# Memory products of the second layer placed beside two norms of the first, and sums over x shared between VectorE and TensorE

## The chip, the cores and the metric

The kernel runs on one core of one Trainium2 chip. The metric is device microseconds of one launch, the median of several runs. A core has TensorE (PE in the rows; its weight loads are PEld), VectorE (DVE), ScalarE (ACT), GpSimd (POOL) and SyncE (SP), which here issues nearly all DMAs.

## The reference

One sequence of 256 tokens with 1024 features goes through a first block of two layers and then a second block of two layers. All is float32. The change touches the first block alone:

```python
x = layer_norm(x, emb_ln_g, emb_ln_b)                                   # norm 0
for l in range(2):
    x = layer_norm(alpha * x + hybrid_mixer(x, ...), ...)               # norm 1, norm 4
    x = layer_norm(alpha * x + memory_cross_attention(x, mem, ...), ...)  # norm 2, norm 5
    x = layer_norm(alpha * x + conv_ffn(x, ...), ...)                   # norm 3, norm 6

def memory_cross_attention(x, mem, xa_q, xa_kv, xa_o):                  # 4 heads of 256
    q = x @ xa_q * 256 ** -0.5
    k, v = split(mem @ xa_kv, 2)
    return (softmax(q @ k.T) @ v) @ xa_o
```

`k` and `v` are made from `mem`, which no layer changes, so these products of either layer depend on nothing that the first block computes. A layer norm needs, for each token, the sum over features of x and of x squared.

## The kernel before

Activations stand transposed, features on partitions: x is 128 x 8 x 256, held as four banks of 128x512. Every large product is cut into chunks, one for each weight piece of 1 MB (128x2048 float32). `plan` (line 105) writes the list of chunks, and all engines walk that list. For a chunk SP loads `raw` (ring of 5), ACT rounds it to `whi` (line 747), DVE subtracts to get `wlo` (line 1537), and PE makes three matmuls for each piece of 128x128 (hi by hi, hi by lo, lo by hi): 48 matmuls of 256 columns. So a chunk that PE multiplies at a given place was split some three chunks earlier (`LEAD`). A chunk may carry hooks: small pieces of other PE work issued ahead of one of its eight steps k.

The chunks of a layer: the mixer (`dq`, `dk`, ... `gate`, `branch`), then `mo` (ends with norm 1 or 4), then the memory attention: `xk` and `xv` (four each, the memory products, which read `memh` and `meml`), `xq` (four, which read the normed x), `xo` (four, which end with norm 2 or 5), then the feed-forward part `fu`, `fg`, `fo` (ends with norm 3 or 6). In both layers the order behind norm 1 or 4 is xk0 xv0 xk1 xv1 xq0 xk2 xq1 xk3 xq2 xq3 xv2 xv3: four memory products stand between the norm and the first chunk that needs its result. Behind norms 2 and 3 stands at once a chunk that needs it (`fu` 0; `dq` 0 of layer 1).

A layer norm runs through all engines:

1. DVE adds each of the four banks of product and x (line 1581). ACT squares each (line 771), DVE adds the squares (line 1574, `acc`).
2. PE sums over partitions by matmuls with ones (`norm_stats`): eight of 256 columns for x into `turnP`, two for `acc` and two for the last squares into `outP`. A float32 matmul shows as two instructions in the trace.
3. DVE takes each token's own sums (1663, 1665), makes mean and variance (1671 to 1673), POOL the power -0.5 (689), DVE two diagonals (1680, 1686), PE spreads them over the partitions (`norm_spread`).
4. For each bank DVE makes `cen` (1633, 1639), ACT the new x and its upper part `xh` (812, 816), and the lower part `xl` is made by DVE for the first bank (1653) and by POOL for the other three (694).

Where memory products follow (norms 1 and 4), `norm_stats` is a hook of the first of them (k = 5) and `norm_spread` one of the second (k = 1), and ACT and DVE make one split (`between`) ahead of the small statistics and one (`late`) ahead of the banks. Elsewhere PE issues both at once and waits, and the split comes behind the norm.

A head of the memory attention takes four steps: `scores` on PE, then its maximum on DVE and exponents on ACT; `turn`, transposes on PE and a copy `eT` on ACT (line 938); `mix`, PE, then a scaling on DVE; `back`, transposes on PE, then a split on ACT and DVE. Head j has its `scores` at the chunk of `xq` j plus 2, and each further step one chunk later.

Of the kernel before, what the change touches and what calls it, by code (L numbers as in the profile page):

```python
# [104 lines left out]
def plan():  # L105
# [15 lines left out]
    for l in range(DEPTH):  # L121
        base = len(chunks)
# [37 lines left out]
        add("M", "mem", l)  # L160
# [6 lines left out]
        for r, j in (("xk", 0), ("xv", 0), ("xk", 1), ("xv", 1), ("xq", 0), ("xk", 2), ("xq", 1), ("xk", 3),  # L167
                     ("xq", 2), ("xq", 3), ("xv", 2), ("xv", 3)):
            where[r, j] = add("T" if r == "xv" else "F", r, l, j)
# [4 lines left out]
        chunks[-1]["ends"] = norm  # L174
        for j in range(FG + 1):
# [17 lines left out]
        for pos, some in todo.items():  # L193
            steps[pos] = sorted(some, key=lambda s: order[s[0]])
# [34 lines left out]
def kernel_program(nc, xT, memT, consts, consts2, pos, par1, par2, bias, W, out):  # L229
# [3 lines left out]
    with ctx:  # L233
# [39 lines left out]

        part1 = ExitStack()
# [4 lines left out]
        qr = sb("qr", [P, 4, S], where=att)  # L279
        kr = sb("kr", [P, 4, S], where=att)  # L280
        qb = sb("qb", [P, 4, S], where=att)
        kb = sb("kb", [P, 4, S], where=att)
        va = sb("va", [P, 2, 512], where=att)
        vb = sb("vb", [P, 2, 512], where=att)
        att.close()
# [5 lines left out]
        hold = ExitStack()  # L291
        _skip = sb("skip_att", [P, 30 * 256], where=hold)
        gates = sb("gates", [P, 3, 4, S], where=hold)
        gbv = sb("gbv", [P, 2, S], where=hold)
        gcv = sb("gcv", [P, 2, S], where=hold)
        pc = sb("pc", [P, 2, S + 2], where=hold)
        cv = sb("cv", [P, 2, S], where=hold)
        mtmp = sb("mtmp", [P, 4, S], where=hold)
        hold.close()
# [7 lines left out]
        kx = sb("kx", [P, KT, S], where=xat)  # L307
        vx = sb("vx", [P, 2, D], where=xat)
# [6 lines left out]
        oxs.close()  # L315
        ff = ExitStack()
        fu = sb("fu", [P, 2, 512], where=ff)
# [7 lines left out]

        cc = sb("cc", [P, NC2], where=ff)
        cs2 = sb("cs2", [P, 2, S], where=ff)
        angle = sb("angle", [P, 2, S], where=ff)
        csr = angle
        posf = sb("posf", [P, S], where=ff)  # L330
        posi = sb("posi", [P, S], mybir.dt.int32, ff)
        q2 = sb("q2", [P, 2, 2, S], where=ff)
        k2 = sb("k2", [P, 2, 2, S], where=ff)
        v2 = sb("v2", [P, 2, 512], where=ff)
        up = sb("up", [P, 2, S], where=ff)
        pooled = sb("pooled", [P, 2, S], where=ff)
# [115 lines left out]
        norms = list(range(LAST + 1))  # L452
        ended = [n for n in norms if n not in (0, END1 + 1)]
# [5 lines left out]
        summed = sig("summed", [(n, b) for n in norms for b in range(1, NB - 1)])  # L459
        ystats = sig("ystats", [n for n in norms if n <= END1])  # L460
# [271 lines left out]
        def _(act):  # L732
# [41 lines left out]
            def norm(n, between=None, late=None):  # L774
# [12 lines left out]
                if between and (n > END1 or n % LNS == 1):  # L787
                    between()
# [32 lines left out]
                if between and n <= END1 and n % LNS != 1:  # L821
                    between()
# [5 lines left out]
            def take(c, pos):  # L828

                r, j, l = c["role"], c["j"], c["l"]  # L830
                if "ends" in c:

                    if c["role"] == "sd" and c["f"] == 0:
# [3 lines left out]
                         (lambda: split_at(pos + 3)) if c["role"] == "mo" else None)  # L837
# [258 lines left out]
        def _(pe):  # L1096
# [9 lines left out]
            def norm_stats(n):  # L1106

                outB.claim(pe, varied, n)
                if n <= END1:
                    turnB.claim(pe, ysums, n)  # L1110
                    for k in range(KT):
                        if k % 2 == 0:
                            await_x(pe, n, k // 2)
                        ins = mm(turnP[:, 0:S], ones[:, :], x[:, k, :], k == 0, k == KT - 1)
# [1192 lines left out]
```

## Time and profile before

| | us |
|---|---|
| median of 3 runs (lowest, highest) | 2185.16 (2183.87, 2185.5) |
| the profiled execution's own time | 2176.07 |
| its span in the trace | 2174.3 |
| PE busy in the span | 2093.7 |
| DVE busy | 1430.6 |
| ACT busy | 1004.3 |

The page gives busy time, then the share of the span. A busy PE is not PE at its peak: matmuls overlap, and the granted clock matters. In the second part of the page the span is cut into 40 slices, with one digit for each:

```profile
PE   7999999899989999998999799998999999999997
...
PEclk9999999999999999999999899999999999999999
DMA  5444554355534444534555355533555555533552
```

PE is at nine tenths or more nearly everywhere; the dips belong to the start, the norms and the end.

### The profile page before, as it was taken

The page shows a single profiled execution, that of the slowest core. Times are in us where ns is not written, and L with a number is a line of the kernel's source. Part 1 is how long each engine was busy: PE and PEld are TensorE (multiplying, and loading weights), DVE is VectorE, ACT ScalarE, POOL GpSimd, SP SyncE. Part 2 cuts the span into 40 slices and gives each one's busy share as a digit, 9 for nine tenths or more (in the row PEclk, how much of TensorE's full clock was granted, in tenths as well). Part 3 has the DMA queues.
Part 4 walks back from the last instruction along what each step waited for, and adds up shares of the span by engine and source line. Part 5 has one row for each costly group of instructions (what it writes and reads, how often), then busy time and mean ns, then how long its engine had stood idle before and what let it go on. Part 6 is the DMA issues. An engine that isn't in the chain of part 4 may idle for free.

```text
span 2174.3 us, 39332 instructions
## 1 busy us (share of the span) xinstructions
PE 2093.7 (96%) x17364; PEld 2038.1 (94%) x17364; DVE 1430.6 (66%) x1717; ACT 1004.3 (46%) x1166; POOL 53.2 (2%) x58
## 2 busy tenths in 40 slices
PE   7999999899989999998999799998999999999997
PEld 6899999899988999998999799988999999989997
DVE  6656564577765655646777766698666766887664
ACT  5554454444445444544444454444444544444442
POOL 1000000000000000001000000000000000000000
PEclk9999999999999999999999899999999999999999
DMA  5444554355534444534555355533555555533552
GB/s 206 151 160 159 190 177 154 117 194 194 194 120 155 156 175 175 192 139 147 193 194 194 104 193 195 190 136 119 194 194 194 180 194 192 178 130 132 194 195 83
DMA packets 52858, 365.95 MB, mean 168 GB/s; under 512 B 5904, under 2 KB 5904, under 8 KB 9296
## 3 DMA queue, kind: packets, MB, share of 16 engines
q1 hardware_dynamic: 52272, 361.21, 46.5%
q8 instruction: 138, 2.26, 0.4%
q0 software_dynamic: 416, 2.22, 0.3%
q14 instruction: 32, 0.26, 0.0%
HBM read 362.35 MB, written 1.05 MB: 167 GB/s over the span
## 4 chain that ended last, share of the span: by engine, by line
PE 82%; issue 9%; DVE 5%; ACT 2%; POOL 1%; DMA 1%; POOLq 0%; ACTq 0%
PE accM L1104 47%; PE scoreP L1104 18%; PE outP L1104 8%; PE turnP L1104 8%; DVE wlo L1537 1%; PE turnP L1284 1%; ACT ew L932 1%; ACT whi L747 1%; POOL small L689 1%; ACT x L812 0%; DMA raw<-in_W 0%; PE outP L1310 0%; DVE cen L1633 0%; DVE mrs L2076 0%; DVE cen L1639 0%
## 5 line engine op out<-in xcount | busy, mean ns | idle before, releaser
L1537 DVE TENSOR_TENSOR wlo<-raw,whi 128x2048 fp32r<-128x2048 f32 x336 | 768.4, 2290 | 379.7 <-ACT whi L747 379.1
L747 ACT ACTIVATE whi<-raw 128x2048 fp32r<-128x2048 f32 x336 | 640.1, 1911 | 261.9 <-PE accM L1104 143.6
L1104 PE MATMUL accM<-xh,whi 128*128 128x256 f32 x1152 | 337.2, 293 | 11.2 <-DVE xl L1653 10.7
L1104 PE MATMUL scoreP<-xh,whi 128*128 128x256 f32 x1152 | 323.1, 280 | 13.7 <-DVE xl L1653 8.8
L1104 PE MATMUL accM<-xh,wlo 128*128 128x256 f32 x1152 | 322.8, 280 | 0.0
L1104 PE MATMUL accM<-xl,whi 128*128 128x256 f32 x1152 | 322.8, 280 | 0.0
L1104 PE MATMUL scoreP<-xl,whi 128*128 128x256 f32 x1152 | 321.2, 279 | 0.0
L1104 PE MATMUL scoreP<-xh,wlo 128*128 128x256 f32 x1152 | 320.9, 279 | 0.0
L1104 PE MATMUL accM<-fh,wlo 128*128 128x256 f32 x1056 | 291.5, 276 | 0.0
L1104 PE MATMUL accM<-fh,whi 128*128 128x256 f32 x1056 | 291.5, 276 | 0.0
L1104 PE MATMUL accM<-fl,whi 128*128 128x256 f32 x1056 | 291.5, 276 | 0.0
L1104 PEld LDWEIGHTS accM<-xh,whi 128*128 128x128 f32 x1152 | 218.2, 189 | 23.7 <-issue 22.8
L1104 PEld LDWEIGHTS scoreP<-xh,whi 128*128 128x128 f32 x1152 | 219.4, 190 | 14.7 <-issue 14.0
L1104 PEld LDWEIGHTS accM<-xl,whi 128*128 128x128 f32 x1152 | 218.1, 189 | 2.6 <-issue 2.4
L1104 PEld LDWEIGHTS accM<-xh,wlo 128*128 128x128 f32 x1152 | 219.7, 191 | 0.0
L1104 PEld LDWEIGHTS scoreP<-xl,whi 128*128 128x128 f32 x1152 | 219.4, 190 | 0.2
L1104 PEld LDWEIGHTS scoreP<-xh,wlo 128*128 128x128 f32 x1152 | 219.5, 191 | 0.0
L1104 PEld LDWEIGHTS accM<-fl,whi 128*128 128x128 f32 x1056 | 198.2, 188 | 0.0
L1104 PEld LDWEIGHTS accM<-fh,whi 128*128 128x128 f32 x1056 | 198.2, 188 | 0.0
L1104 PEld LDWEIGHTS accM<-fh,wlo 128*128 128x128 f32 x1056 | 198.2, 188 | 0.0
L1104 PE MATMUL turnP<-xh,whi 128*128 128x256 f32 x480 | 132.5, 276 | 0.0
L1104 PE MATMUL turnP<-xl,whi 128*128 128x256 f32 x480 | 132.5, 276 | 0.0
(273 smaller groups left out, 4161.0 us busy)
## 6 DMA issues: line engine op xcount, KB each, us to landing
raw<-in_W SPq DMA_DIRECT2D x336, 1024.0 KB, 4.8
biasr<-in_bias SPq DMA_DIRECT2D x16, 256.0 KB, 2.8
raw<-in_memT SPq DMA_DIRECT2D x2, 1024.0 KB, 5.4
cc<-in_consts POOLq DMA_DIRECT2D x1, 1408.0 KB, 6.8
x<-in_xT SPq DMA_DIRECT2D x4, 256.0 KB, 4.5
out<-x SPq DMA_DIRECT2D x4, 256.0 KB, 2.6
c<-in_consts SPq DMA_DIRECT2D x1, 464.5 KB, 6.8
par<-in_par POOLq DMA_DIRECT2D x2, 203.5 KB, 3.6
```

The source lines that it names most:

```text
L689: nc.gpsimd.tensor_tensor(root, var, mhalf, ALU.pow).then_inc(rooted.sem, 1)
L747: nc.scalar.activation(whi[:, hi_slot(c), :], raw[:, raw_slot(c), :], ACT.Copy).then_inc(split_hi.sem, 1)
L932: ins = nc.scalar.activation(ew[:, e0 + i, :], src, ACT.Exp, bias=negmax[:, e0 + i:e0 + i + 1], scale=scale, accum_out=rsum[:, s0 + i:s0 + ...
L1104: return nc.tensor.matmul(dst, a, b, start=start, stop=stop, skip_group_check=True)
L1284: ins = nc.tensor.transpose(turnP[:, k * S + t * P:k * S + (t + 1) * P], src[t][:, k * P:(k + 1) * P], ident)
L1537: v.tensor_tensor(wlo[:, raw_slot(c), :], raw[:, raw_slot(c), :], whi[:, hi_slot(c), :].bitcast(F32), ALU.subtract).then_inc(split_lo.sem, 1)
```

## The change

`plan` puts xk0 and xv0 of layer 1 behind norm 2, and xk1 and xv1 of layer 1 behind norm 3, both of which lie ahead of layer 1's mixer. In layer 1 what remains is xk2 xv2 xk3 xq0 xq1 xq2 xq3 xv3. The places of a layer 1 head's steps follow `xq`, and there `mix` moves into the chunk of `turn`, and `back` one chunk earlier. The norms with a memory product behind them are now called `covered`: 1, 2, 3 and 4. They take the hooks and the split `between`; behind `xo` and `fo` the second split comes ahead of the banks on ACT, behind them on DVE (`brief`). In a covered norm DVE adds banks 0, 1 and 2 of x (`add_tokens`, into `cen`), and PE sums that sum and bank 3: four matmuls with ones where there were eight. In every norm the fourth square waits for the first sum of squares where it waited for the second. `kx` and `vx` get a place of their own in SBUF, so other tiles move.

```diff
     for l in range(DEPTH):
+        if l:
+            for r, j in (("xk", 1), ("xv", 1)):
+                add("T" if r == "xv" else "F", r, l, j, mem=mem)
...
+            close = kind == "xa" and l == 1
             at(pos, "scores", h)
             at(pos + 1, "turn", h)
-            at(pos + 2, "mix", h)
+            at(pos + 2 - close, "mix", h)
             if last:
-                at(pos + 3, "back", h)
+                at(pos + 3 - close, "back", h)
...
-        for r, j in (("xk", 0), ("xv", 0), ("xk", 1), ("xv", 1), ("xq", 0), ("xk", 2), ("xq", 1), ("xk", 3),
-                     ("xq", 2), ("xq", 3), ("xv", 2), ("xv", 3)):
+        order = (...) if l == 0 else \
+            (("xk", 2), ("xv", 2), ("xk", 3), ("xq", 0), ("xq", 1), ("xq", 2), ("xq", 3), ("xv", 3))
...
+        if l == 0:
+            for r, j in (("xk", 0), ("xv", 0)):
+                add("T" if r == "xv" else "F", r, 1, j, mem=mem)
...
+        covered = [c["ends"] for c in chunks if "ends" in c and c is not chunks[-1]
+                   and chunks[c["c"] + 1]["role"] == "xk"]
...
                 if b >= 2:
-                    act.wait_ge(summed.sem, summed.at((n, b - 1)))
+                    act.wait_ge(summed.sem, summed.at((n, 1)))
...
-                         (lambda: split_at(pos + 3)) if c["role"] == "mo" else None)
+                         (lambda: split_at(pos + 3)) if c["ends"] in covered else None)
...
+                    if n in covered:
+                        pe.wait_ge(xsummed.sem, xsummed.at((n, 2)))
+                        for h in range(2):
+                            mm(turnP[:, 0:S], ones[:, :], cen[:, 0, h * S:(h + 1) * S], h == 0, False)
+                        await_x(pe, n, NB - 1)
+                        for h in range(2):
+                            ins = mm(turnP[:, 0:S], ones[:, :], x[:, KT - 2 + h, :], False, h == 1)
...
-                if c["role"] == "mo":
+                if n in covered:
                     hook(pos + 1, 5, lambda n=n: norm_stats(n))
                     hook(pos + 2, 1, lambda n=n: norm_spread(n))
...
+                def add_tokens(b):
+                    if b == 1:
+                        for d in range(2):
+                            await_x(dve, n, d)
+                        v.tensor_tensor(cen[:, 0, :], flat(0), flat(1), ALU.add).then_inc(xsummed.sem, 1)
+                    else:
+                        await_x(dve, n, 2)
+                        dve.wait_ge(xsummed.sem, xsummed.at((n, 1)))
+                        v.tensor_tensor(cen[:, 0, :], cen[:, 0, :], flat(2), ALU.add).then_inc(xsummed.sem, 1)
...
+                    if n in covered and b >= 2:
+                        add_tokens(b - 1)
...
+                    brief = c["role"] in ("xo", "fo")
                     norm(c["ends"], lambda: split_at(pos + 2),
-                         (lambda: split_at(pos + 3)) if c["role"] == "mo" else None)
+                         (lambda: split_at(pos + 3)) if c["ends"] in covered and not brief else None)
+                    if c["ends"] in covered and brief:
+                        split_at(pos + 3)
```

On PE at norm 2 the program before has, behind the last matmul of `xo` 3, both rounds of the norm and then `fu` 0 (it writes `scoreP`):

```order
L1104 MATMUL accM<-oh,wlo 128x256
L1104 MATMUL turnP<-x,ones 128x256 x8
L1104 MATMUL outP<-acc,ones 128x256 x2
L1104 MATMUL outP<-sq,ones 128x256 x2
L1104 MATMUL turnP<-diag,ones 128x128 x2
L1104 MATMUL outP<-diag,ones 128x128 x2
L1104 MATMUL scoreP<-xh,whi 128x256
```

The changed program has the first round inside xk0 of layer 1 (`accM<-memh,...`):

```order
L1120 MATMUL accM<-memh,wlo 128x256
L1120 MATMUL turnP<-cen,ones 128x256 x2
L1120 MATMUL turnP<-x,ones 128x256 x2
L1120 MATMUL outP<-acc,ones 128x256 x2
L1120 MATMUL outP<-sq,ones 128x256 x2
L1120 MATMUL accM<-memh,whi 128x256
```

Five steps of that chunk stand ahead of it; the second round stands inside xv0, behind its first step, and seven steps follow before `fu` 0.

On DVE at norm 2, the program before, from the third residual to the spread result (`diag` rows are the tokens' own sums):

```order
L1581 SCALAR_TENSOR_TENSOR x<-x,accM 128x512 x3
L1574 TENSOR_TENSOR acc<-sq 128x512
L1581 SCALAR_TENSOR_TENSOR x<-x,accM 128x512
L1574 TENSOR_TENSOR acc<-acc,sq 128x512
L1663 TENSOR_TENSOR diag<-turnP,c0 128x2x128
```

The changed program at the same place:

```order
L1617 SCALAR_TENSOR_TENSOR x<-x,accM 128x512 x3
L1606 TENSOR_TENSOR cen<-x 128x512
L1597 TENSOR_TENSOR acc<-sq 128x512
L1617 SCALAR_TENSOR_TENSOR x<-x,accM 128x512
L1610 TENSOR_TENSOR cen<-cen,x 128x512
L1597 TENSOR_TENSOR acc<-acc,sq 128x512
L1560 TENSOR_TENSOR wlo<-raw,whi 128x2048
L1701 TENSOR_TENSOR diag<-turnP,c0 128x2x128
```

Two adds and one split have come in ahead of the statistics. At the end of the same norm the changed program has, behind the last bank (`cen`), a split of a chunk that ACT has rounded already, and then the next one:

```order
L1691 TENSOR_TENSOR xl<-x,xh 128x512
L1671 TENSOR_TENSOR cen<-x,turnP 128x512
L1677 TENSOR_TENSOR cen<-cen,outP 128x512
L1560 TENSOR_TENSOR wlo<-raw,whi 128x2048 x2
L2209 MEMSET fgp 128x4 x2
```

Before, one split stood there, behind the one that ACT made after its own norm.

On ACT, memory attention of layer 1, the changed program at `xq` 3, the first chunk with `turn` and `mix` together:

```order
L842 ACTIVATE qx<-accM 128x512
L948 ACTIVATE ew,rsum<-scoreP,negmax 128x256 x2
L763 ACTIVATE whi<-raw 128x2048
L954 ACTIVATE eT<-turnP 128x512
L842 ACTIVATE qx<-accM 128x512
```

The copy `eT`, for which `mix` of the same chunk waits, stands behind a split.

## Rows read from the trace of the kernel before

**Rows 1.** part 1 of the page: busy us, share of the span, instructions

```profile
PE 2093.7 (96%) x17364; PEld 2038.1 (94%) x17364; DVE 1430.6 (66%) x1717; ACT 1004.3 (46%) x1166; POOL 53.2 (2%) x58
```

**Rows 2.** windows: us, busy (x) of PE, PEld, DVE, ACT, POOL; PEclk, DMA, GB/s

```profile
290.00:403.00 113.00, 112.79 (x898) 110.24 (x898) 59.76 (x69) 53.24 (x68) 4.62 (x4) 1.00 0.43 152
403.00:431.00 28.00, 20.64 (x135) 19.46 (x134) 16.13 (x28) 14.37 (x20) 4.58 (x4) 0.82 0.22 76
431.00:599.00 168.00, 168.00 (x1484) 168.00 (x1484) 123.32 (x134) 81.20 (x75) 0.00 (x0) 1.00 0.55 195
599.00:629.00 30.00, 22.34 (x153) 20.69 (x152) 19.27 (x34) 16.45 (x21) 5.16 (x5) 0.89 0.30 101
```

**Rows 3.** chain of waits, norm 2: start us, us, engine, tile, line, count

```profile
402.91 3.45 PE turnP L1104 x16
406.36 1.74 PE outP L1104 x8
...
411.03 0.91 PE turnP L1104 x4
...
416.48 0.61 DVE xl L1653
...
417.23 2.90 PE scoreP L1104 x12
```

**Rows 4.** chain of waits, norm 3

```profile
599.06 3.45 PE turnP L1104 x16
...
613.17 8.91 PE accM L1104 x64
```

**Rows 5.** chain of waits over the whole span: the products behind norm 2

```profile
417.23 13.19 PE scoreP L1104 x96
430.42 5.44 PE turnP L1104 x48
```

**Rows 6.** windows, columns as in rows 2, inside norm 2 and behind norm 3

```profile
410.00:417.23 7.23, 1.78 (x9) 1.55 (x9) 5.64 (x13) 3.22 (x6) 0.37 (x1) 0.59 0.00 1
...
613.17:616.00 2.83, 2.83 (x13) 2.83 (x14) 1.14 (x2) 2.77 (x7) 2.29 (x2) 0.50 0.02 6
```

**Rows 7.** chain of waits, norm 1

```profile
289.83 3.66 PE accM L1104 x30
293.50 3.45 PE turnP L1104 x16
...
298.71 0.44 DVE diag L1663
...
301.62 0.68 PE turnP L1104 x4
```

**Rows 8.** timeline, norm 1, DVE and ACT: start, us, engine, line, tiles [idle]

```profile
289.60 0.68 DVE L1574 TENSOR_TENSOR acc<-sq 128x512 f32<-128x512 f32 x1
...
294.30 2.29 DVE L1537 TENSOR_TENSOR wlo<-raw,whi 128x2048 fp32r<-128x2048 f32 x1 [2.56 <-ACT whi L747]
...
292.37 3.69 ACT L747 ACTIVATE whi<-raw 128x2048 fp32r<-128x2048 f32 x2
```

**Rows 9.** timeline, end of norm 2, DVE and POOL

```profile
417.71 0.69 DVE L1639 TENSOR_TENSOR cen<-cen,outP 128x512 f32<-128x512 f32 x1
...
420.71 1.30 POOL L694 TENSOR_TENSOR xl<-x,xh 128x512 fp32r<-128x512 f32 x1 [0.35 <-ACT xh L816]
```

**Rows 10.** timeline, a norm of the second part, DVE and POOL

```profile
1407.38 2.29 DVE L1537 TENSOR_TENSOR wlo<-raw,whi 128x2048 fp32r<-128x2048 f32 x1
...
1407.55 2.66 POOL L689 TENSOR_TENSOR small<-small 128x2 f32<-128x2 f32 x1 [186.76 <-DVE small L1675]
```

**Rows 11.** POOL's power, all 14: ns min/median/max

```profile
L689 POOL TENSOR_TENSOR small<-small x14: 690/692/2663, 13.6 to 2164.7; 128x2 f32<-128x2 f32 x14
```

**Rows 12.** timeline, memory attention of layer 1, ACT

```profile
929.98 0.58 ACT L938 ACTIVATE eT<-turnP 128x512 f32<-128x512 f32 x1
```

**Rows 13.** part 6 of the page: weight loads, KB each, us to landing

```profile
raw<-in_W SPq DMA_DIRECT2D x336, 1024.0 KB, 4.8
```

More of the change, by code:

```diff
@@ L166, in plan @@
         where = {}
[L167 to L169 removed]
+        order = (("xk", 0), ("xv", 0), ("xk", 1), ("xv", 1), ("xq", 0), ("xk", 2), ("xq", 1), ("xk", 3),
+                 ("xq", 2), ("xq", 3), ("xv", 2), ("xv", 3)) if l == 0 else \
+            (("xk", 2), ("xv", 2), ("xk", 3), ("xq", 0), ("xq", 1), ("xq", 2), ("xq", 3), ("xv", 3))
+        for r, j in order:
+            where[r, j] = add("T" if r == "xv" else "F", r, l, j, mem=mem)
         chunks[where["xq", 0]]["norm"] = norm
@@ L193, in plan @@
         for pos, some in todo.items():
-            steps[pos] = sorted(some, key=lambda s: order[s[0]])
+            behind = [s for s in some if s[0] == "mix" and s[1]["kind"] == "xa" and l == 1]
+            steps[pos] = sorted([s for s in some if s not in behind], key=lambda s: order[s[0]]) + behind
     norm += 1
@@ L272, in kernel_program @@
         otok = sb("otok", [P, 2, S])
+        kvs = ExitStack()
+        kx = sb("kx", [P, KT, S], where=kvs)
+        vx = sb("vx", [P, 2, D], where=kvs)
         part1 = ExitStack()
@@ L459, in kernel_program @@
         summed = sig("summed", [(n, b) for n in norms for b in range(1, NB - 1)])
+        xsummed = sig("xsummed", [(n, b) for n in covered for b in (1, 2)])
         ystats = sig("ystats", [n for n in norms if n <= END1])
@@ L786, in norm @@
                         square(n, b)
-                if between and (n > END1 or n % LNS == 1):
+                if between and (n > END1 or n in covered):
                     between()
@@ L820, in norm @@
                         upper(n + 1, b)
-                if between and n <= END1 and n % LNS != 1:
+                if between and n <= END1 and n not in covered:
                     between()
@@ L1110, in norm_stats @@
                     turnB.claim(pe, ysums, n)
[L1111 to L1114, printed above, removed]
+                    if n in covered:
[6 more added lines that the diff above has]
+                    else:
+                        for k in range(KT):
+                            if k % 2 == 0:
+                                await_x(pe, n, k // 2)
+                            ins = mm(turnP[:, 0:S], ones[:, :], x[:, k, :], k == 0, k == KT - 1)
                     ins.then_inc(ystats.sem, 1)
@@ L1612, in norm @@
                 norm_front(n)
-                if between and not rms and n % LNS == 1:
+                if between and not rms and n in covered:
                     between()
@@ L1656, in norm @@
                     lo_part(n + 1, NB - 1)
-                if between and n <= END1 and n % LNS != 1:
+                if between and n <= END1 and n not in covered:
                     between()
```

55 lines of the change are left out of this document (29 added, 26 removed).

## The prediction, made before the changed kernel ran

> **What bounds the kernel now.** I read the page's engine shares first, then windows of time, then the chain of waits inside the norms, then timelines of single engines. PE is busy 2093.7 of 2174.3 us [rows 1], and its instructions take most of the chain, so only PE's idle stretches and its slow ones can be won. The windows show where they are. The stretch from norm 1 to norm 2, 113 us with a covered norm in it, leaves PE idle for 0.2 us. The 28 us around norm 2 leave it idle for 7.4 us at a mean clock of 0.82, the 30 us around norm 3 for 7.7 us at 0.89. The feed-forward stretch between them has none: 168.00 of 168.00 us [rows 2].
>
> Inside norm 2 the chain shows this. PE ends `xo` 3 at 402.91, sums x for 3.45 us and the squares for 1.74, waits for the small statistics until 411.03, and waits again until DVE has the first `xl` (416.48 plus 0.61) before `fu` 0 starts at 417.23: 14.32 us without a product [rows 3]. Norm 3 takes 613.17 - 599.06 = 14.11 us [rows 4]. The clock is granted at 0.59 in the last 7 us of norm 2 and at 0.50 in the first 2.8 us of products behind norm 3, the lower level, 1.2 GHz [rows 6]. So the first 96 matmuls behind norm 2 take 13.19 us, where 48 take 5.44 at full clock [rows 5]: 2.3 us lost. Behind norm 3 64 take 8.91 us, at full clock 7.25: 1.7 us lost [rows 4, 5].
>
> **Norms 2 and 3, the two products.** I count from r, the moment when PE enters the cover; a product is 5.44 us [rows 5]. PE's work in the norm is now 1.73 (half of 3.45, four sums for eight) + 1.74 in the first round [rows 3], and in the second 0.68 for `turnP` [rows 7] and about 0.6 for `outP`. PE comes to the second round at r + 5.44 + 3.47 + 0.68 = r + 9.6.
> The other engines: in norm 1 ACT begins its pair of `whi` at 292.37, DVE the `wlo` at 294.30, ending 296.5 [rows 8], which is r + 6.7 (r = 289.83 [rows 7]). DVE's two adds of x cost about what `acc` costs, 0.68 each [rows 8] (0.6 back to back), but the fourth square no longer waits for the second `acc`, which gives that back; I keep r + 6.5. Then DVE takes the tokens' own sums of x, two instructions of 0.44 [rows 7], to r + 7.4, and from there to PE's second round it is 301.62 - 298.71 = 2.91 us [rows 7]: r + 10.1 or a bit more. PE waits 0.5 us there. From the end of the `turnP` half (411.94) to the first product it was 5.3 us [rows 3], so the first bank stands at r + 10.1 + 0.7 + 5.3 = r + 16.1. PE arrives at r + 10.1 + 1.27 + 7/8 x 5.44 = r + 16.1: level. So `fu` 0 starts 16.1 - 14.32 = 1.8 us later than before, `dq` 0 2.0 later, with two products (10.88 us) done.
> Then `fu` 0 is paced by its banks: POOL ends the last `xl` 1.30 us after 420.71 [rows 9], 4.9 us behind the first of DVE (417.09), so one bank comes each 1.64 us; with the last quarter of the product that makes 6.4 us. Before, `fu` 0 took 13.19 - 5.44 = 7.75 us and `dq` 0 8.91 - 1.81 = 7.1 us, on the slow clock [rows 4, 5]. That is 1.35 and 0.7 us won.
> Norm 2: 10.88 - 1.8 + 1.35 = 10.4 us; norm 3: 10.88 - 2.0 + 0.7 = 9.6 us.
>
> **A split beside POOL's `xl`.** Behind `xo` and `fo` DVE makes a split directly after its last `cen`; that ends 1.3 us after the first `xl` [rows 3, 9], and ACT rounded the piece long before. Before, no `wlo` ran beside an `xl` of POOL. One row shows what happens then: a `wlo` at 1407.38 for 2.29 us, and POOL's power, started at 1407.55, takes 2.66 us and ends 0.5 us behind it [rows 10]; its median is 0.69 [rows 11]. So POOL stood still for DVE. Here the second `xl` of POOL (ready 2.0 us behind the first bank) meets a `wlo` that ran from 1.6 (POOL's first `xl` done) to 3.9; I put its end at 5.05 in place of 3.3, the third's at 6.4 in place of 4.9. `fu` 0 and `dq` 0 end 1.5 us later, 3.0 us in all. The bounds are 0 (they don't meet) and 2.29 each.
> The Trainium skill ("SBUF — State Buffer", summary) says that a VectorE instruction with two SBUF inputs and a GpSimd instruction that reads SBUF exclude each other, the second to issue blocking fully. By that rule, and rows 10 agree, the loss is there and the sum is 19.3; without it 22.3.
>
> **Norms 1 and 4, the sums.** The work of PE falls by 1.73 us each. But the statistics start at r + 7.4 in place of 298.71 - 289.83 = 8.9, so PE's second round comes 1.5 us sooner and the rest is waiting. 3.0 us for both; the bounds are 3.5 and, if DVE's two adds delay everything, 0.
> Norm 4 keeps three products of its four. PE then wants `xq` 0 at r + 3 x 5.44 + 3.47 + 1.27 = r + 21.1; the first bank, with the late split of 2.2 us ahead of it, is there at r + 10.1 + 0.7 + 2.2 + 5.3 = r + 18.3. Nothing is lost. In layer 1's later attention the products removed are the same that were added, so their PE time is already in the count.
>
> **The heads of layer 1.** `turn` and `mix` now share a chunk. With three hooks `mix` stands at k = 5, some 2.0 us behind the transposes. ACT frees itself from the exponents about 3.65 us into the chunk, makes a `whi` (1.85 [rows 8]), then `eT` (0.58 [rows 12]): 6.1, where PE is at 5.7. With four hooks both meet at 7.0. Four heads: I take 0.7 us lost, bounds 0 and 9.8 (each head a whole `whi` and `eT`, 4 x 2.45).
> `whi` and `wlo` of `fg` 0, `dk` 0 and of the pieces behind come up to 4 us later against PE than before; the tightest, `dk` 0, is ready some 1 us ahead. The moved tiles, the earlier wait of the fourth square in the norms of the second part (there the second `acc` ends last) and the weight loads (the same 336) I cost at nothing; the loads land in 4.8 us where PE needs one each 5.44 [rows 5, 13].
>
> **Sum.** 10.4 + 9.6 - 3.0 + 3.0 - 0.7 = 19.3 us. The profiled execution took 2176.07 us (its span 2174.3, with 1.8 around it), so it would take 2156.8. The median of the runs is 2185.16, 9.1 above the profiled one; I carry that over: 2165.9 us.
>
> **Rivals.**
> - *The two don't meet*: POOL's `xl` and the split pass each other, or share. For it: the row of the clash is of POOL's power, not of an `xl`. Against: that it stood still there at all [rows 10]. 22.3 us, 2162.9.
> - *The clock falls inside `fu` 0 and `dq` 0*, where PE now waits some 2 us for the third bank, right behind two shorter waits. For it: the clock was already low at the end of norm 2 [rows 6]. Against: norm 1 has short waits too, and its stretch shows 1.00 [rows 2]. The price is what the slow clock cost before, 2.3 + 1.7: 15.3 us, 2169.9.
> - *The heads wait at the bound*: 9.8 in place of 0.7, 10.2 us, 2175.0. For it: ACT's split stands between the transposes and `eT`; against: ACT is busy 46% [rows 1].
> - *The change doesn't do what it says*: the covered norm lengthens by what it covers, since DVE and ACT can't do split, statistics and banks in the time, and only the sums' 3.0 us are left: 2182.2. Against: norm 1 does exactly this at no idle time [rows 2].
> - *Slower*: the loads become the bound. Norms 2 and 3 are pauses in which the ring of weights refills; without them the 78 chunks from norm 2 to norm 4 need one load each 5.44 us. From a landing of 5.44 + 19.3/78 = 5.7 us on the gain is gone; at 5.8 the price is 28 us, 2194. Against: 168 us of unbroken work at 195 GB/s with the DMA engines 0.55 busy [rows 2].
>
> **How the numbers follow.** Forecast 0.55; not meeting 0.17; clock 0.15; heads 0.06; does nothing 0.03; slower 0.04. The likeliest is 2165.9. Its own range, by the bounds of the split (0 to 4.6), of the sums and of 0.5 us of waits, is 2163 to 2169. The range for 8 in 10 is 2160.5 to 2175: it holds the first three cases and the edge of the fourth, with 2 us for the step from one session's median to another's. About 0.2%, 4.4 us, is what a measurement of this kernel can tell from no change. Faster by more: the first four, 0.93; within: 0.03; slower: 0.04.
>
> **What would show it.** In the changed profile PE's idle time around norms 2 and 3 should fall from 7.4 and 7.7 us to some 3 each, with a clock near 1.00; `turnP` sums 1.7 us in place of 3.45; in the same norms a POOL `xl` of about 3 us in place of 1.30 beside a `wlo` of 2.29, and a wait of PE for `xl` of some 2 us; norms 1 and 4 with a PE wait for `diag` of 0.4 us. It would be wrong if `fu` 0 waited for `wlo`, if the clock in the 28 us from norm 2 on stayed under 0.95, or if PE waited over 1 us for an `eT`.

## The result, and the profile after

| | time, us | span of the profiled execution | its own time |
|---|---|---|---|
| before | 2184.51 median of 4 runs (2181.32 to 2185.5) | 2174.3 | 2176.07 |
| after | 2154.41 median of 4 runs (2152.04 to 2156.35) | 2152.6 | 2154.44 |

The ratio is 0.9862, with a 95% interval of 0.9826 to 0.9898: 30.1 us less between the medians, 21.6 us less between the two profiled executions. Forecast were 19.3 us of gain and a median of 2165.9. The measured 2154.41 lies below the stated range. For the profiled execution the working gave 2156.8; it took 2154.44. So the sum of the mechanism's terms (19.3 for 21.6 us) is 2.3 us off, and the other 9 us come from one other step.

The page after, part 1, answers [rows 1]:

```profile
PE 2085.7 (97%) x17332; PEld 2030.7 (94%) x17332; DVE 1435.0 (67%) x1725; ACT 1002.7 (47%) x1166; POOL 56.4 (3%) x58
```

32 matmul instructions are gone, 8 (four float32 matmuls) in each of the covered norms 1 to 4, and PE is idle for 66.9 us in place of 80.6.

Windows of after, columns as in [rows 2]. The stretches are cut anew around the same norms, so their lengths differ from those of before:

```profile
280.00:403.00 123.00, 122.51 (x989) 120.03 (x988) 68.35 (x77) 57.14 (x73) 4.62 (x4) 1.00 0.46 163
403.00:431.00 28.00, 26.16 (x209) 25.22 (x208) 22.14 (x31) 18.01 (x22) 6.19 (x4) 1.00 0.42 152
431.00:603.00 172.00, 172.00 (x1520) 172.00 (x1519) 124.90 (x137) 84.40 (x78) 0.00 (x0) 1.00 0.55 194
603.00:635.00 32.00, 30.14 (x237) 28.74 (x237) 25.71 (x35) 18.28 (x23) 6.77 (x5) 1.00 0.43 150
```

Norm 2 leaves PE idle for 1.84 us where it was 7.4, norm 3 for 1.86 where it was 7.7, and the granted clock is 1.00 in both (before: 0.82 and 0.89). The feed-forward stretch between them still has no idle time.

The chain of waits of after in norm 2, against [rows 3]: start us, us, engine, tile, line, count.

```profile
405.44 1.73 PE turnP L1120 x8
407.17 1.74 PE outP L1120 x8
408.91 0.02 issue
408.93 0.44 DVE diag L1701
...
411.84 0.70 PE turnP L1120 x4
...
418.91 0.64 ACT xh L832
419.55 0.07 issue
419.62 2.94 POOL xl L710
422.56 0.04 issue
422.61 8.45 PE scoreP L1120 x72
```

The sums of x take 1.73 for 3.45 us. Between PE's sums and the first product the norm lies on DVE, ACT and POOL, as before, but PE has two products beside it. Apart from its spread at 411.84 PE shows in the chain again only behind POOL's `xl`, for which it waits. The timeline of the same place, PE, DVE and POOL (start, us, engine, line, tiles, idle before):

```profile
401.87 0.28 PE L1120 MATMUL accM<-memh,whi 128*128 128x256 f32 x1
...
417.90 0.28 PE L1120 MATMUL scoreP<-xh,whi 128*128 128x256 f32 x1
...
422.61 0.38 PE L1120 MATMUL scoreP<-xh,whi 128*128 128x256 f32 x1 [1.63 <-POOL xl L710]
```

```profile
418.86 2.57 DVE L1560 TENSOR_TENSOR wlo<-raw,whi 128x2048 fp32r<-128x2048 f32 x1
```

```profile
417.97 1.31 POOL L710 TENSOR_TENSOR xl<-x,xh 128x512 fp32r<-128x512 f32 x1 [6.79 <-ACT xh L832]
419.62 4.19 POOL L710 TENSOR_TENSOR xl<-x,xh 128x512 fp32r<-128x512 f32 x2 [0.34 <-ACT xh L832]
```

PE enters the cover at 401.87 (r) and starts `fu` 0 at 417.90, r + 16.0; r + 16.1 was forecast. POOL's second `xl` lies beside DVE's split (418.86 to 421.43) and takes 2.94 us where its first takes 1.31; it ends 1.1 us behind the split's end. All 18 `xl` of POOL, min/median/max in ns:

```profile
L710 POOL TENSOR_TENSOR xl<-x,xh x18: 1286/1308/2942, 23.2 to 991.3; 128x512 fp32r<-128x512 f32 x18
```

Place by place, by milestones in both traces (the same instruction before and after; products that the change does early are counted where they are done):

| place | forecast, us | between the traces, us |
|---|---|---|
| up to norm 1 | 0 | -0.6 |
| norm 1, its sums | 1.5 | 1.6 |
| norm 2 | 10.4 - 1.5 = 8.9 | 9.2 |
| norm 3 | 9.6 - 1.5 = 8.1 | 8.5 |
| norm 4 and the heads of layer 1 | 1.5 - 0.7 = 0.8 | 0.9 |
| behind it | 0 | 2.0 |
| sum | 19.3 | 21.6 |

### The profile page after: what moved, and what is told of

It is laid out like the page before. It is cut to its first block, busy times and chain, and to the rows that moved or that the text cites. A ratio compares the mean times of both kernels' runs of the same rounds, so it can differ in the third digit from the quotient of the medians.

```text
span 2152.6 us, 39281 instructions
## 1 busy us (share of the span) xinstructions
PE 2085.7 (97%) x17332; PEld 2030.7 (94%) x17332; DVE 1435.0 (67%) x1725; ACT 1002.7 (47%) x1166; POOL 56.4 (3%) x58
## 4 chain that ended last, share of the span: by engine, by line
PE 83%; issue 9%; DVE 4%; ACT 2%; POOL 1%; DMA 0%; POOLq 0%; ACTq 0%
PE accM L1120 48%; PE scoreP L1120 18%; PE outP L1120 8%; PE turnP L1120 8%; DVE wlo L1560 1%; PE turnP L1307 1%; ACT x L828 1%; ACT ew L948 1%; PE outP L1333 0%; ACT whi L763 0%; DVE mrs L2117 0%; ACT xh L832 0%; DVE cen L1671 0%; POOL xl L710 0%; POOL small L705 0%
## 5 line engine op out<-in xcount | busy, mean ns | idle before, releaser
L1120 PE MATMUL accM<-xh,whi 128*128 128x256 f32 x1152 | 336.8, 292 | 8.2 <-DVE xl L1691 6.5
L1120 PE MATMUL scoreP<-xh,whi 128*128 128x256 f32 x1152 | 322.3, 280 | 10.7 <-DVE xl L1583 4.9
L1120 PE MATMUL accM<-xl,whi 128*128 128x256 f32 x1152 | 322.5, 280 | 0.0
L1120 PE MATMUL accM<-xh,wlo 128*128 128x256 f32 x1152 | 322.5, 280 | 0.0
L1120 PE MATMUL scoreP<-xl,whi 128*128 128x256 f32 x1152 | 320.3, 278 | 0.0
L1120 PE MATMUL scoreP<-xh,wlo 128*128 128x256 f32 x1152 | 320.2, 278 | 0.0
L1120 PE MATMUL accM<-fh,wlo 128*128 128x256 f32 x1056 | 291.5, 276 | 0.0
L1120 PE MATMUL accM<-fh,whi 128*128 128x256 f32 x1056 | 291.5, 276 | 0.0
L1120 PE MATMUL accM<-fl,whi 128*128 128x256 f32 x1056 | 291.5, 276 | 0.0
L1120 PEld LDWEIGHTS accM<-xh,whi 128*128 128x128 f32 x1152 | 217.7, 189 | 20.7 <-issue 18.3
L1120 PEld LDWEIGHTS scoreP<-xh,whi 128*128 128x128 f32 x1152 | 218.7, 190 | 11.8 <-issue 9.2
L1120 PEld LDWEIGHTS accM<-xl,whi 128*128 128x128 f32 x1152 | 217.7, 189 | 2.6 <-issue 2.4
L1120 PEld LDWEIGHTS accM<-xh,wlo 128*128 128x128 f32 x1152 | 219.2, 190 | 0.0
L1120 PEld LDWEIGHTS scoreP<-xl,whi 128*128 128x128 f32 x1152 | 218.5, 190 | 0.2
L1120 PEld LDWEIGHTS scoreP<-xh,wlo 128*128 128x128 f32 x1152 | 218.5, 190 | 0.0
L1120 PEld LDWEIGHTS accM<-fh,wlo 128*128 128x128 f32 x1056 | 198.2, 188 | 0.0
L1120 PEld LDWEIGHTS accM<-fl,whi 128*128 128x128 f32 x1056 | 198.2, 188 | 0.0
L1120 PEld LDWEIGHTS accM<-fh,whi 128*128 128x128 f32 x1056 | 198.2, 188 | 0.0
L1120 PE MATMUL turnP<-xh,whi 128*128 128x256 f32 x480 | 132.5, 276 | 0.0
L1120 PE MATMUL turnP<-xl,whi 128*128 128x256 f32 x480 | 132.5, 276 | 0.0
```

Of the source, the lines that this page charges most:

```text
L1120: return nc.tensor.matmul(dst, a, b, start=start, stop=stop, skip_group_check=True)
```

## The experiments

Medians are of the runs taken beside runs of the kernel before on the same chip; the interval is that of the ratio. The last two columns come from each run's trace and are explained under e1. The interval of e1, which is the kernel before against itself, does not hold 1, so a ratio that lies 0.3% from 1 shows nothing of an edit.

| run | median, us | ratio to before | span of the profile | long stretches at 117.8 ns | net span |
|---|---|---|---|---|---|
| before, first profile | | | 2174.3 | 0 | 2162.2 |
| e1, before again | 2190.02 | 1.0033 [1.0012, 1.0055] | 2182.4 | 1 | 2163.1 |
| e11, before a third time | 2185.49 | 1.0017 [0.999, 1.0045] | 2191.6 | 3 | 2158.4 |
| after, first profile | | 0.9862 [0.9826, 0.9898] | 2152.6 | 0 | 2139.2 |
| e2, after again | 2159.77 | 0.9914 [0.9881, 0.9946] | 2157.9 | 1 | 2138.7 |
| e10, after a third time | 2160.08 | 0.99 [0.9875, 0.9925] | 2159.6 | 1 | 2139.1 |
| e3, moves only | 2170.54 | 0.9945 [0.992, 0.997] | 2161.5 | 0 | 2148.1 |
| e4, sums only | 2176.74 | 0.9971 [0.995, 0.9992] | 2183.1 | 2 | 2156.5 |
| e5, square only | 2184.62 | 0.9999 [0.9971, 1.0027] | 2181.3 | 1 | 2161.4 |
| e6, POOL first | 2166.16 | 0.9923 [0.9897, 0.9949] | 2164.3 | 2 | 2137.8 |
| e7, `xl` on DVE | 2165.37 | 0.9926 [0.9897, 0.9954] | 2154.0 | 1 | 2135.4 |
| e12, the same again | 2160.34 | 0.991 [0.9881, 0.9938] | 2157.2 | 1 | 2136.9 |
| e8, heads as before | 2175.3 | 0.9965 [0.9941, 0.999] | 2167.0 | 1 | 2147.9 |

### e1 and e2: both kernels again, unchanged

> The kernel before, unchanged, run again for its times, granted clock and one more trace. The step of the prediction in doubt is the one from the profiled execution (2176.07 us) to the median (2185.16): the traces alone differ by 21.6 us, near the forecast of 19.3, the medians by 30.1. Theory A (the clock differs from execution to execution, by where short idle stretches fall): the runs spread from about 2175 to 2186 us, and the slower ones show a lower mean granted clock, by some 0.001 for each 1 to 2 us; the ratio to the kernel before is 1.000. Theory B (the chip or the session sets an offset): all runs of one call lie within 1 to 2 us of each other, at 2176 or at 2185, with the same clock.

> The changed kernel, unchanged, beside the kernel before on one chip in five rounds. Theory A: the gain is 21.6 us (two traces) plus what the clock does on average, 25 to 31 us in all, ratio 0.986 to 0.989, and its runs have a mean clock some 0.003 to 0.006 higher than those of the kernel before. Theory B: on one chip the gain is that of the traces, 19 to 22 us, ratio 0.990, and the clocks differ by the 0.003 of the two traces.

The same program came out at 2181.55 to 2203.07 us in 12 runs, and the kernel before, beside it, at 2174.49 to 2192.37 in 30. Theory A fails on the clock: the mean granted clock of these 42 runs is 0.983 to 0.987, for short and long ones alike. Theory B fails on the spread. No wait of PE is over 0.5 us longer in e1's trace. What differs is the pace of PE. The chain of waits behind norm 5, first the kernel before, then e1:

```profile
1020.83 5.44 PE turnP L1104 x48
1026.27 5.44 PE outP L1104 x48
1031.71 5.44 PE accM L1104 x48
```

```profile
1022.26 5.65 PE turnP L1104 x48
1027.91 5.65 PE outP L1104 x48
1033.57 5.65 PE accM L1104 x48
```

And the window 1022:1189 of the two, columns as in [rows 2]:

```profile
1022.00:1189.00 167.00, 167.00 (x1476) 167.00 (x1475) 122.29 (x134) 81.24 (x74) 0.00 (x0) 1.00 0.55 196
```

```profile
1022.00:1189.00 167.00, 167.00 (x1421) 167.00 (x1420) 118.59 (x129) 78.85 (x73) 0.00 (x0) 1.00 0.52 187
```

In both PE is busy for all of 167.00 us at a granted clock of 1.00, yet one execution gets 1476 matmuls through and the other 1421: 113.3 against 117.8 ns from one to the next. The transfers are lower with it (187 for 196 GB/s), as PE takes fewer pieces; in neither trace does PE wait inside the window. The pace is one and the same for the whole stretch, and changes only where PE stops or its stream changes. There are six such stretches of some 32 products, each from one norm to the next (behind norms 2 and 5, and four in the second part), and one at the long pace costs 6.7 to 7.0 us. The stretches of the mixers' gates run at 117.8 ns in every trace of the table. The span less what all matmuls at the long pace take over 113.3 ns I call the net span: 2162.2 and 2163.1 for the kernel before, 2139.2 and 2138.7 for the changed one. By these four traces the change is worth 23 to 24 us; with e11's, below, 19 to 24. e2 came out at the 0.990 that theory B gave, but its runs spread over 22.5 us.
Times from norm to norm in the following are net in the same way. They are shorter than in the trace as it stands, above all from norm 3 to norm 4, where the mixer's gates lie: 283.8 us as it stands, 278.7 net.

### e3, e4 and e5: the change in parts

e3 is the changed kernel without the adds of x and with the old wait of the fourth square:

```diff
-                    act.wait_ge(summed.sem, summed.at((n, 1)))
+                    act.wait_ge(summed.sem, summed.at((n, b - 1)))
...
-                    if n in covered:
+                    if False:
...
-                    if n in covered and b >= 2:
-                        add_tokens(b - 1)
```

> The chunks moved and the norms covered, but TensorE sums all eight parts of x in every norm, VectorE adds no banks of x, and the fourth square waits as before. The prediction's own terms: norms 2 and 3 keep about their gain, less up to 1.5 us each since the statistics come 1.7 us later while the start of the first product is level between TensorE and the banks; norms 1 and 4 give back 1.5 each: 4 to 6 us slower than the full change. Rival (the adds are worth only TensorE's own time in the two norms with slack): 3 us slower. Rival (the adds on VectorE cost what they save): no difference within 1 us.

e4 is the kernel before with those adds in norms 1 and 4 and the early wait; e5 is it with the early wait alone:

```diff
+        covered = [1, 4]
...
-                    act.wait_ge(summed.sem, summed.at((n, b - 1)))
+                    act.wait_ge(summed.sem, summed.at((n, 1)))
...
+                    if n in covered and b >= 2:
+                        add_tokens(b - 1)
```

> No chunk moved: the kernel before with VectorE's two adds in norms 1 and 4, four matmuls with ones there in place of eight, and the earlier wait of the fourth square in every norm. By the prediction 3.0 us faster than before (the change's trace shows 1.6 for norm 1). If more than 5 us are gained, the wait of the fourth square in the norms of the second part is worth something, which I costed at nothing; if the moves alone and this one do not add up to the full change, the rest is the clock's.

> The kernel before with one edit: in every norm the fourth square waits for the first sum of squares in place of the second. I costed it at nothing. In the traces so far the stretch from the sums of the sixth to those of the seventh norm of the second part (the last layer's mixer) takes 107.4 to 107.8 us without the edit and 105.4 to 105.6 with it. Theory (the edit sets the moment of TensorE's pauses there and so how long it runs at 1.2 GHz): that stretch again 105.4 to 105.6 us, some 2 us less, all others as before. Rival (it comes from the work ahead, shifted in time): 107.4 to 107.8. Over the whole, apart from stretches at 5.65 us a product, 2 us faster or 0.

The moves alone give 14.1 us of net span, the sums with the early wait 5.7, together 19.8 of 23.0; in the medians 0.9945 and 0.9971. e3 is 8.9 us of net span longer than after, where 4 to 6 were expected, and e4 gains more than the 5 us from which the wait was to be worth something. In e3 the segment from norm 1 to norm 2 takes 112.0 us for 110.2 in after, the next two 199.2 for 197.5 and 281.7 for 278.7: fewer sums on PE and the earlier wait together pay 1.7 to 3 us in each norm, also in those with two products beside them. The early wait alone does not do it: in e5 the same three segments are not shorter than before. In e3's norm 2 DVE, done with its split, waits for both of PE's sums; in after it waits for neither:

```profile
410.99 0.42 DVE L1699 TENSOR_TENSOR diag<-turnP,c 128x256 f32<-128x256 f32 x1 [0.55 <-PE turnP L1120]
...
412.72 0.42 DVE L1699 TENSOR_TENSOR diag<-outP,c 128x256 f32<-128x256 f32 x1 [0.85 <-PE outP L1120]
```

The early wait alone can't be told from nothing in the medians (0.9999). In its trace the last layer's mixer takes 104.6 us for 106.7, with the granted clock at 1.00 for 0.97, but other segments are up to 0.6 us longer and the net span is only 0.8 us shorter. That mixer was my explanation of the 2.0 us "behind it". e11 took half of it back (below).
The low clock is not gone either. In the mixer of the second block's first layer the granted clock is 1.00 before and 0.95 in the changed kernel. First before, then after:

```profile
1404.00:1510.40 106.40, 99.84 (x751) 88.48 (x750) 93.21 (x181) 47.41 (x83) 3.35 (x2) 1.00 0.34 121
```

```profile
1384.40:1491.40 107.00, 103.03 (x751) 90.91 (x750) 92.49 (x180) 47.33 (x84) 3.35 (x2) 0.95 0.34 121
```

That mixer is 0.6 us longer with it. Low clock stands there in 8 of all 12 traces with the early wait (e5 among them, 0.95) and in none of the 4 without; by chance such a split has a probability of 0.04.

### e6 and e7: the split beside POOL's `xl`

e6 makes DVE wait for POOL's last `xl` before the split; e7 makes the third and fourth `xl` on DVE in norms 2 and 3 and lets the split come behind them.

```diff
+                        dve.wait_ge(xlo1.sem, xlo1.at((c["ends"], NB - 1)))
```

```diff
...
+                if n in (2, 3):
+                    for b in (2, 3):
+                        dve.wait_ge(xhi.sem, xhi.at((n, b)))
+                        k = slice(2 * b, 2 * b + 2)
+                        v.tensor_tensor(xl[:, k, :], x[:, k, :], xh[:, k, :].bitcast(F32), ALU.subtract)\
+                            .then_inc(xlo3.sem, 1)
```

> The changed kernel, but behind xo and fo VectorE waits for GpSimd's last xl before it splits. Theory (the split kept GpSimd's second and third xl waiting): all GpSimd xl take 1.3 us, TensorE's waits of 1.6 us for them fall to 0.2 or less, and the split ends 7.2 us behind the first xl, so fg 0 and dk 0 start some 0.7 us earlier than now and not 1.5: 1 to 1.5 us faster in all. Rival (both are slow for another reason, such as the moved tiles): an xl of 2.9 us stays.

> The changed kernel, but in norms 2 and 3 VectorE makes the lower parts of the third and fourth bank of x (0.69 us each in place of 1.30 on GpSimd) and then the split. Theory: no xl of 2.9 us, fu 0 and dq 0 end 2.1 us earlier; the split ends 6.5 us behind the first xl, fg 0 and dk 0 then wait some 0.7 us for it: 2.5 to 3 us faster in all. Rival (the split is now what bounds): a wait of over 1.5 us for wlo in each and no gain.

All `xl` of POOL in e6:

```profile
L710 POOL TENSOR_TENSOR xl<-x,xh x18: 1288/1304/1313, 24.3 to 991.0; 128x512 fp32r<-128x512 f32 x18
```

With no split beside it the instruction never takes more than 1.31 us, so the 2.94 are the split's doing, as the theory said. PE's wait of 1.6 us for `xl` is gone, and one for `wlo` has come, in e6's waits inside 400:440:

```profile
PE scoreP L1120 <- DVE wlo L1560: 0.7, 1, 0.7
```

So parting the two gains only the difference, 0.9 us, at that spot, and from norm 2 to norm 3 e6 takes 197.1 us for 197.5, where 1 to 1.5 us were expected for both norms. In e7 PE's wait at `fu` 0 falls from 1.6 us for `xl` to 0.3 for `wlo`; 2.5 to 3 us were expected. It is 1.2 us shorter than after from norm 2 to norm 3 (196.3 for 197.5) and 0.8 from norm 3 to norm 4 (277.95 for 278.73). Neither shows in the medians, where the pace of a single stretch is worth seven times that.

### e8: the heads of layer 1 at the old distances

```diff
-            close = kind == "xa" and l == 1
+            close = False
...
-            behind = [s for s in some if s[0] == "mix" and s[1]["kind"] == "xa" and l == 1]
+            behind = []
```

> The previous kernel with layer 1's heads at the old distances: mix two chunks behind scores, back three. The fourth head's back then stands ahead of xo 3, which needs it. Theory of the prediction (turn and mix in one chunk cost 0.7 us): the waits inside the chunks vanish, but xo 3 waits for back, ScalarE and VectorE, some 1.5 to 2 us: 1 us slower. Rival (sharing a chunk costs up to 9.8 us): faster by several us.

From norm 4 to norm 5 it takes 96.66 us where the changed kernel takes 87.64: with four products fewer to lie between a head's steps, PE comes to `outP` too soon, before DVE has read a head's last step out of it into `ol`. Of e8's waits of PE:

```profile
PE outP L1120 <- DVE ol L2156: 6.1, 3, 3.0
```

6.1 us in three waits, the longest 3.0. A fourth, of `xo` 3 for `ol`, takes 1.5, as expected of it, and the granted clock falls to 0.91 in the 20 us from 940 on; in after it is 1.00 there. Expected was 1 us in all: the three waits were not foreseen. Drawing `turn` and `mix` into one chunk is therefore no cost of the change but a condition of it. The median is 2175.3, and the net span 8.7 us longer.

### e9, e13 and e14: what sets the pace

The changed kernel with a short extra matmul ahead of each F product, of 64 columns in e9, 32 in e13 and 128 in e14; the matmul behind it overwrites its result.

```diff
+                                if first:
+                                    mm(dst[:, 0:64], w_hi, a_hi[:, k, 0:64], True, False)
                                 mm(o, w_hi, a_hi[:, k, :], first, False)
```

> The changed kernel with one extra matmul of 64 columns ahead of the first matmul of each F product (about 210 of them; its result is overwritten by the matmul behind it). By its columns it costs 64/256 of 113 ns, 28 ns, so about 6 us in all and a net span near 2145. Asked is what sets the pace of an undisturbed stretch of products, 5.44 us (113.3 ns a matmul) or 5.65 us (117.7). Theory A, the pace is set anew at each small break in the stream: inside one long feed-forward stretch of this kernel products of 5.44 and of 5.65 us alternate in a mixed row, each execution has about the same mixture, and the timed runs lie within 5 us of each other. Theory B, the pace holds through such breaks until PE really stands still: each long stretch is still of one pace throughout and the runs still lie on steps of about 6.7 us, over a spread of 15 us or more. Theory C, the pace is a matter of the chip's moment and not of the program: the same as B here, but the three kernels of this call would show slow stretches at the same places.

| | median (lowest to highest), us | share at 117.8 ns in the long stretches |
|---|---|---|
| e9, 64 columns | 2200.96 (2199.95 to 2201.99), 6 runs | 0.68 to 0.70 in five, 0.59 in one |
| e13, 32 columns | 2204.99 (2204.72 to 2205.78), 4 runs | 0.63 to 0.65 in four, 0.84 in two |
| e14, 128 columns | 2190.44 (2188.71 to 2193.0), 10 runs | 0.32 to 0.34 in five, 0.70 in one |

The chain of waits of e9 inside one long stretch:

```profile
1045.31 5.57 PE turnP L1120 x49
1050.88 5.76 PE outP L1120 x49
1056.64 5.65 PE accM L1120 x48
1062.30 11.34 PE scoreP L1120 x98
1073.63 5.44 PE accM L1120 x48
```

Theory A holds. Products of 5.44 and 5.65 us stand side by side in one stretch, so at each short matmul the pace is set anew: the product at 1056.64 runs at 117.8 ns, the one at 1073.63 at 113.3. And with 212 such breaks the times of one program lie within 2.0 us of each other in e9, where those of the kernel before, run beside it, spread over 28.8. The price was misjudged: a break costs some 115 ns and not 28 (the matmul behind the short one starts 29 ns after it, and the next one 199 ns later, where without it one gap of 113 stands), some 24 us for the 212 of them. The rest of the 41 us over e10 I put down to the larger share of the long pace.

> The kernel with the extra short matmuls, these now of 32 columns in place of 64 (their results are overwritten). With 64 columns the two gaps around each were 29 and 199 ns, and 115 ns is what one break costs; about 70 in 100 matmuls of the long stretches then ran at 117.7 ns. Theory A, the length of the break decides which pace follows: the share at 117.7 becomes another one, below 30 or above 90 in 100. Theory B, the break draws the pace whatever its length: again 60 to 80 in 100, and the time is 2198 to 2203. In both the runs lie within 3 us of each other.

> The same with 128 columns: 57 ns by its columns in place of 28, so 6 us more than with 64 for the same mixture of paces (2207). Theory A, the length decides: a share at 117.7 ns other than 60 to 80 in 100, each tenth of the long stretches' matmuls being worth about 4 us in all. Theory B, whatever its length: 60 to 80 in 100 and 2204 to 2210.

In e14 theory A holds in five of six stretches, whose share lies outside 0.60 to 0.80, and the time lies under B's 2204. In e13 neither is met as written: four stretches stay inside 0.60 to 0.80, as B asked, two do not, and none comes under 0.30 or over 0.90, as A asked. The share does change with the length of the break. Chain of waits of e14, two rounds of the same three products:

```profile
1044.10 5.58 PE turnP L1120 x49
1049.68 5.76 PE outP L1120 x49
1055.44 5.65 PE accM L1120 x48
1061.09 11.34 PE scoreP L1120 x98
1072.43 5.65 PE accM L1120 x48
1078.09 5.58 PE turnP L1120 x49
1083.66 5.76 PE outP L1120 x49
1089.43 5.65 PE accM L1120 x48
```

The pattern repeats from round to round and differs between the lengths, so I take it that the pace that follows a break depends on its timing. Timing against what, no run here shows. A version that holds 113.3 ns throughout was not found; e14, the best of the three, has a median 30 us above e10's.

### e10 to e12: after, before and e7 a third and second time

> The changed kernel, unchanged, a third time. By the theory that the executions of one program differ by long stretches at 117.7 in place of 113.3 ns a matmul, its span less 6.7 us for each long stretch at the slow pace is 2139 +- 1 as in the two traces before, and its fastest run lies near 2151 to 2154. Against the kernel before, the ratio is 0.989 +- 0.003 (a net gain of 23 to 24 us). If the difference between executions lies elsewhere, the span less the slow stretches differs from 2139 by more than 2 us.

> The kernel before, unchanged, a third time. By the same theory its span less the slow stretches is 2162.5 +- 1, its fastest run lies near 2173 to 2176, and the ratio is 1.000 +- 0.003. The prediction took the distance of the profiled execution (2176.07) from the median of its runs (2185.16) as a fixed 9.1 us; by the theory it is a matter of how many long stretches were slow, so here it will be another number, between -10 and +10.

> The version in which VectorE also makes the third and fourth xl in norms 2 and 3, a second time. Net of slow stretches it was 2 us shorter than the changed kernel (1.2 behind norm 3's bank and 0.8 behind norm 4's). If that is real, its net span is 2137 +- 1 and its ratio against the kernel before 0.988 +- 0.003; its fastest run lies 2 us below the fastest of the changed kernel in this call. If it was chance, the two are level.

e10 met its expectation, but for its fastest run of 2155.14. Its chain of waits shows one long stretch at 117.8 ns, where the changed kernel's first trace has `1498.00 5.44 PE turnP L1120 x48`:

```profile
1498.83 5.65 PE turnP L1120 x48
1504.48 5.65 PE outP L1120 x48
```

The runs of the kernel before beside these lie in groups, as steps of one stretch would have it: 9 at 2175.6 to 2178.3, 3 at 2181.9 to 2183.5, 4 at 2189.1 to 2191.0, 1 at 2204.4. The 30 runs beside e1 and the 28 beside e5 don't part so clearly, and only profiled executions show their stretches.
e11 has three long stretches at 117.8 ns, but its net span is 2158.4, 4 us below what I expected. 1.8 of these are the last layer's mixer, 104.9 us with the clock at 1.00, in a kernel that has the old wait of the fourth square; for the rest I have no cause. The windows of that mixer as they stand, gates at the long pace included, first before, then e11:

```profile
1885.50:1993.10 107.60, 103.03 (x757) 91.34 (x757) 92.94 (x183) 48.54 (x84) 1.38 (x2) 0.97 0.34 119
```

```profile
1898.70:2004.50 105.80, 99.93 (x754) 88.73 (x753) 92.49 (x183) 48.52 (x84) 1.38 (x2) 1.00 0.35 121
```

Over all 16 traces it ran short (104.5 to 105.2 us, net) in 10 of 12 with the early wait and in 1 of 4 without. That such a split comes by chance has a probability of 0.06, so that the early wait helps there is likely and not shown.
e12 repeats e7: 196.5 us for 197.5 from norm 2 to norm 3, 277.5 for 278.8 to norm 4; net span 2136.9, as expected. Its fastest run is level with e10's (2155.02 and 2155.14) and not 2 us below it. It is the best version by the traces, by about 2 us. In the medians of one session it and the changed kernel are level, 2160.34 and 2160.08, and the interval can't tell them apart.

## Why the prediction was right or wrong

**What bounds the kernel, right.** PE's idle and slow time around norms 2 and 3 was what could be won, and it was won there: 17.7 of 21.6 us.

**Norms 2 and 3, right.** Forecast 8.9 and 8.1 behind the split's price, measured 9.2 and 8.5. `fu` 0 starts at r + 16.0, for r + 16.1, PE reaches the second round at r + 10.0, for r + 10.1. That agreement is in part luck: the working's own terms, 7.4 + 2.91, make 10.3, and DVE was done with the sums of x at r + 7.1. Other slips of the working are of 0.1 us: 294.30 + 2.29 is 296.6 and not 296.5, 4.9 and a quarter of 5.44 are 6.3 and not 6.4, and 4 x (1.85 + 0.58) is 9.7 and not 9.8. The clock is 1.00, so rival 2 (the clock falls) is out, and so is the one that the covered norm lengthens.

**The split beside `xl`, right.** 2.94 us beside a split against 1.31 alone, and in e6 none over 1.31. POOL's second `xl` ended 4.9 us behind the first bank (417.63), for 5.05. But what can be got back by parting them is 0.9 us of PE's waits in each norm and not 1.5 (0.4 in e6's segment from norm 2 to norm 3), since the split must then wait.

**Sums in norms 1 and 4, right in the first profile.** 1.6 for 1.5 in norm 1. The wait for `diag` is 0.2, as it was before the change, and not 0.4. The working used the four sums in norms 2 and 3 too, but gave them no price of their own: e3, without them and without the early wait, is 8.9 us of net span longer, 2.0 of it in the last mixer.

**Heads of layer 1, right.** From norm 4 to norm 5 before took 108.57 and after 87.64 us with four products fewer; 4 x 5.44 - 20.93 is 0.8 us lost, for 0.7. e8 shows what the new order avoids.

**"... I cost at nothing", in part wrong.** The earlier wait of the fourth square stood in that sentence. 2.0 us came behind norm 5: the last mixer is 2.0 us shorter, and that of the layer ahead of it, where the clock is now 0.95, is 0.6 longer (e5). Whether the wait brought this or chance is the open point of e11. The loads did not become the bound: they land in 4.8 us as before, at 194 GB/s.

**The step that failed: "The median of the runs is 2185.16, 9.1 above the profiled one; I carry that over".** I took the distance between the profiled execution and the median as a constant of the kernel. In the traces of this kernel the place of an execution follows mainly from how many of its long stretches run at 117.8 ns: 0, 1 and 3 of them with spans of 2174.3, 2182.4 and 2191.6, and 0 in the profiled execution that I started from. For the three runs behind the median of 2185.16 there is no trace, so that they had such stretches is inferred. e1's and e11's profiled executions are 2184.17 and 2193.4, their medians 5.9 above and 7.9 below them. The changed kernel's four first runs lie within 2.4 us of its profiled execution, which had none either. Without the 9.1 the forecast is 2156.8, 2.4 from the measured 2154.41. The range failed with it: it had 2 us for the step between sessions, where one program's runs spread over 18 to 31. That the three runs of before lay within 1.6 us of each other was luck, and I read it as accuracy. The 0.2% that the prediction took as the least that can be told from no change was too small as well: e1, the same program, differs from it by 0.33%. By the same token the 30.1 us between the first medians flatter the change; the repeats give 0.9914 and 0.99, 19 to 22 us, and the net spans 19 to 24.

## What to carry to other kernels

Work out a change from one trace against the other, and before carrying a profile over to the median of other runs, count how many matmuls each long stretch gets through at a granted clock of 1.00: here two executions of one program differed by up to three whole stretches. When work is drawn into the shadow of a norm, price the second engine's instructions beside it too, and move what hangs on the old distance between steps with it (here `mix`, 9 us). Judge edits of 1 to 2 us by the segments between fixed milestones of several traces, with the long pace taken out, not by medians in which a single stretch weighs 6.7 us or more.

## What the runs showed of the hardware that was not expected

- PE's undisturbed streams of 256-column matmuls have two steady paces at a granted clock of 1.00, 113.3 and 117.8 ns (5.44 and 5.65 us for 48). Of 78 long stretches in 13 traces 14 ran at the longer one; each cost 6.7 to 7.0 us. What sets the pace no run shows. A short matmul in the stream sets the pace anew, in a pattern that depends on its length.
- A single short matmul of 32, 64 or 128 columns costs some 115 ns in the stream, as much as one of 256: in e14 the two gaps behind it are 61 and 167 ns, together 115 more than the 113 without it.
- POOL's subtraction of 128x512 takes 2.94 us with DVE's of 128x2048 beside it and 1.31 without (e6). It ends 1.1 us behind DVE's, so it gets next to nothing done meanwhile; DVE's takes 2.57 for 2.29.
- An edit of one wait that is worth nothing in the medians (0.9999) changed where the granted clock is low: 0.97 in the last mixer and 1.00 in the one ahead of it before, 1.00 and 0.95 with the edit alone (e5). With one trace of it, and e11 at 1.00 in the last mixer without it, the cause is likely and not shown.
